# Linear attention in a two-layer block: level products over all 128 rows with a zeroed key operand, one masked copy a level, and no context outputs in the last layer

## What is computed

```python
def step(state, inp):                       # scanned over chunks, both directions
    qc, kc, vc, gc = inp
    b = jnp.cumsum(gc, axis=2)
    rel = jnp.exp(jnp.where(lower, b[:, :, :, None, :] - b[:, :, None, :, :], -jnp.inf))
    att = jnp.einsum('bhtk,bhsk,bhtsk->bhts', qc, kc, rel)
    o = (jnp.einsum('bhtk,bhkv->bhtv', qc * jnp.exp(b), state)
         + jnp.einsum('bhts,bhsv->bhtv', att, vc))
    ...
oc_f, sc_f = gla_chunked(pc['gq'], pc['gk'], pc['gv'], pc['gf'], zero_state)
ol_f, _ = gla_chunked(pl['gq'], pl['gk'], pl['gv'], pl['gf'], sc_f)
...
gla_lat = gla_output(ol_f + ol_b, pl['go'], gla_norm_g[layer])
if not last:
    gla_ctx = gla_output(oc_f + oc_b, pc['go'], gla_norm_g[layer])
```

## Time and profile before

| | |
|---|---|
| median of 3 runs | 4480.63 us (4475.74 to 4485.02) |
| profiled execution, time and span | 4477.87 us, 4476.0 us |
| mean granted TensorE clock | 0.888 of 2.4 GHz |
| linear attention, layer 0 and layer 1 (first head's diagonal to the last copy's end) | 227.1 and 235.4 us |
| DMA over the span | 71 GB/s |

### The profile page before, as it was taken

One profiled execution on the slowest core, in us unless ns is written; L12 is line 12 of the kernel. 1 busy time (PEld: TensorE's weight loads), 2 busy tenths in 40 slices (PEclk: granted clock), 3 DMA queues, 4 the chain that ended last, 5 costly groups with the idle time before them and its releaser, 6 DMA issues. The chain is left out here.

```text
span 4476.0 us, 53765 instructions
## 1 busy us (share of the span) xinstructions
PE 3734.3 (83%) x20722; PEld 3001.0 (67%) x20722; DVE 1757.0 (39%) x2589; ACT 1242.4 (28%) x2146; POOL 1248.0 (28%) x877
## 2 busy tenths in 40 slices
PE   6899596895786999999976697796959669999992
PEld 2588486673465888888861585685746458888881
DVE  2105543785563221221228014543967442122215
ACT  2211332674533111111004211432746331111111
POOL 1211321122334323323223211321214343333331
PEclk8999676797997999999998898676989879999996
DMA  8322302104332111111115223202021321111112
GB/s 296 135 84 113 87 13 60 26 11 96 89 101 75 38 38 37 37 37 39 36 59 210 95 86 125 48 19 62 19 63 43 127 75 43 55 48 47 47 38 89
DMA packets 150919, 318.59 MB, mean 71 GB/s; under 512 B 11816, under 2 KB 72200, under 8 KB 150768
## 3 DMA queue, kind: packets, MB, share of 16 engines
q1 hardware_dynamic: 128016, 260.47, 18.4%
q10 hardware_dynamic: 18528, 41.97, 2.5%
q0 software_dynamic: 4224, 14.09, 1.1%
HBM read 250.20 MB, written 66.29 MB: 71 GB/s over the span
## 5 line engine op out<-in xcount | busy, mean ns | idle before, releaser
L2006 POOL TENSOR_TENSOR ffn_wlo<-ffn_raw,ffn_whi 128x1024 fp32r<-128x1024 f32 x132 | 314.7, 2392 | 800.1 <-ACT ffn_whi L1977 800.1
L2070 DVE TENSOR_TENSOR ffn_hid<-ffn_up,ffn_silu 128x512 f32<-128x512 f32 (+1 forms) x110 | 70.2, 638 | 1048.9 <-PE ffn_up L127 1022.7
L1977 ACT CAST ffn_whi<-ffn_raw 128x1024 fp32r<-128x1024 f32 x132 | 136.4, 1049 | 944.6 <-PE ffn_acc L127 467.4
L2075 DVE TENSOR_TENSOR y<-ffn_acc,y 128x512 f32<-128x512 f32 x396 | 273.9, 692 | 266.7 <-PE ffn_acc L127 266.7
L125 PE MATMUL ffn_gate<-second_uhi,ffn_whi 128*128 128x512 f32 (+1 forms) x880 | 325.7, 370 | 37.3 <-POOL ffn_wlo L2006 37.3
L126 PE MATMUL ffn_gate<-second_ulo,ffn_whi 128*128 128x512 f32 (+1 forms) x880 | 325.3, 370 | 0.0
L127 PE MATMUL ffn_gate<-second_uhi,ffn_wlo 128*128 128x512 f32 (+1 forms) x880 | 325.1, 369 | 0.0
L126 PE MATMUL ffn_up<-second_ulo,ffn_whi 128*128 128x512 f32 (+1 forms) x880 | 323.9, 368 | 0.0
L125 PE MATMUL ffn_up<-second_uhi,ffn_whi 128*128 128x512 f32 (+1 forms) x880 | 323.8, 368 | 0.0
L127 PE MATMUL ffn_up<-second_uhi,ffn_wlo 128*128 128x512 f32 (+1 forms) x880 | 323.7, 368 | 0.0
L125 PE MATMUL ffn_acc<-ffn_whi,ffn_hhi 128*128 128x512 f32 x792 | 308.2, 389 | 0.0
(11 more groups left out here) (265 smaller groups left out, 8785.6 us busy)
## 6 DMA issues: line engine op xcount, KB each, us to landing
ffn_raw<-w_ffn_dram SPq DMA_DIRECT2D x132, 512.0 KB, 3.3
in_raw<-w_in_dram SPq DMA_DIRECT2D x42, 512.0 KB, 3.3
norm_input_ada_w<-w_ada_dram SPq DMA_DIRECT2D x10, 2048.0 KB, 8.2
norm_ffn_ada_w<-w_ada_dram SPq DMA_DIRECT2D x8, 2048.0 KB, 8.1
proj_scratch<-in_stage ACTq DMA_DIRECT2D x20, 640.0 KB, 2.9
ada_w<-w_ada_dram SPq DMA_DIRECT2D x6, 2048.0 KB
...
```

Of the source, the lines that this page charges most:

```text
L1977: act.copy(whi[:, j % 3, :], raw[:, j % 3, :]).then_inc(w_hi, 1)
L2006: pool.tensor_tensor(wlo[:, j % 3, :], raw[:, j % 3, :], whi[:, j % 3, :].bitcast(F32), ALU.subtract).then_inc(w_ready, 1)
L2070: dve.tensor_tensor(hf[:, c, 0:tn], UP[:, c, 0:tn], sg[:, c, 0:tn], ALU.mult).then_inc(mul_done, 1)
L2075: dve.tensor_tensor(Y[:, tt, cols], ACC[:, half, :], Y[:, tt, cols], ALU.add).then_inc(y_added, 1)
```

## The change

Each level becomes one matmul a chunk over all 128 rows. The moving operand is X as it is, 128 columns. The stationary operand is a copy XK of X in which the queries are set to zero: in the lower halves the rows DOWN, in the upper halves the rows UP. ScalarE makes XK with two activations a level (`key_parts`), each a copy with a scale of one or zero per partition (`side`, set by three small memsets on GpSimd). XK is a ring of 2. The product has the forward and the backward blocks in one 128x128 square per chunk, beside blocks that nothing reads, and takes the unit's banks from their start, so `level` has no wait for a bank. One predicated copy of 128x1280 under a mask of 128x128 takes the blocks of a level into A where two of 128x640 did.

In layer 1 (C0 = 2) levels, diagonal, output, mean, root, gate and store leave out the two context chunks, and so do the distances and exponentials of steps 1 to 4. Keys, states, XAB and the distances of step 0 stay whole, since the states need them.

```diff
+        C0 = CTX_TILES if layer == LAYERS - 1 else 0
+        ASKED = range(C0, NCH)
+        NA, t0 = NCH - C0, C0 * P
...
+        XK = sb(nm + "XK", [P, 2, T])
+        side = sb(nm + "side", [P, 2])
...
-        masks = sb(nm + "masks", [P, 10, HALF], I32)
+        masks = sb(nm + "masks", [P, 5, P], I32)
...
-                    plan(("level", h, l), "dve", 2)
+                    plan(("level", h, l), "dve", 1)
...
-        pieces = [[range(4 * k, min(4 * k + 4, NCH)) for k in range(3)] if g % STEPS == 4 else [range(2 * k, 2 * k + 2) for k in range(PAIRS)]
-                  for g in range(NS)]
+        def pieces_of(p):
+            first, n = (0, 2) if p == 0 else (C0, 4 if p == 4 else 2)
+            return [range(c, min(c + n, NCH)) for c in range(first, NCH, n)]
+        pieces = [pieces_of(g % STEPS) for g in range(NS)]
...
+            pool.memset(side[:, :], 0.0).then_inc(side_set, 1)
+            pool.wait_ge(side_set, 1)
+            pool.memset(side[UP, 0:1], 1.0).then_inc(side_set, 1)
+            pool.wait_ge(side_set, 2)
+            pool.memset(side[DOWN, 1:2], 1.0).then_inc(side_set, 1)
+            pool.wait_ge(side_set, 3)
...
-                for c in range(NCH):
-                    x = X[:, v % RING, chunk(c)]
-                    if c == 8:
-                        pe.wait_ge(bank_left, left(("level", h, l)) + 1)
-                    pe.matmul(fslot(s, c), x[UP, :], halves(x, m)[UP, :, 1, :], start=True, stop=True)
-                    mm = pe.matmul(bslot(s, c), x[DOWN, :], halves(x, m)[DOWN, :, 0, :], start=True, stop=True)
-                    if c == 1:
-                        mm.then_inc(bank_left, 1)
+                pe.wait_ge(key_part, 2 * (v + 1))
+                for c in ASKED:
+                    mm = pe.matmul(U[:, s, chunk(c)], XK[:, v % 2, chunk(c)], X[:, v % RING, chunk(c)], start=True, stop=True)
                 mm.then_inc(unit_done, 1)
...
+            def key_parts(g, k):
+                if g >= NS or k >= len(levels_of(g)):
+                    return
+                h, l = g // STEPS, levels_of(g)[k]
+                m, v = LEVELS[l], level_number(h, l)
+                if v == 0:
+                    act.wait_ge(side_set, 3)
+                act.wait_ge(x_pool, x_count(h, l))
+                act.wait_ge(x_dve, x_count(h, l))
+                if v >= 2:
+                    act.wait_ge(unit_done, made(("level",) + divmod(v - 2, len(LEVELS))))
+                for half in range(2):
+                    act.activation(halves(XK[:, v % 2, t0:], m)[:, :, half, :], halves(X[:, v % RING, t0:], m)[:, :, half, :],
+                                   ACT.Copy, scale=side[:, half:half + 1]).then_inc(key_part, 1)
...
                 h, p = divmod(g, STEPS)
+                key_parts(g, 1)
                 exponential(g + 2, 0)
                 exponential(g + 2, 1)
...
+                key_parts(g + 1, 0)
                 exponential(g + 2, 3)
...
-                shape = [P, NCH, HALF // m, m]
-                for d in range(2):
-                    dve.wait_ge(dve_took, taken(name) - 2 + d)
-                    data = U[:, s, 0:T // 2] if d == 0 else U[:, s, 3 * BANK - T // 2:3 * BANK]
-                    mask = masks[:, 2 * (l - 2) + d:2 * (l - 2) + d + 1, :].rearrange("p a (n m) -> p a n m", m=m).to_broadcast(shape)
-                    dve.copy_predicated(A[:, h % 2, :, :].rearrange("p c (n a m) -> p c n a m", a=2, m=m)[:, :, :, 1 - d, :], mask,
-                                        data.rearrange("p (c n m) -> p c n m", c=NCH, m=m)).then_inc(dve_took, 1)
+                dve.wait_ge(dve_took, taken(name) - 1)
+                mask = masks[:, l - 2:l - 1, :].to_broadcast([P, NA, P])
+                dve.copy_predicated(A[:, h % 2, C0:, :], mask, U[:, s, t0:T].rearrange("p (c n) -> p c n", n=P)).then_inc(dve_took, 1)
```

67 lines of the change are left out of this document (33 added, 34 removed).

## The result

The changed kernel takes **4347.92 us** (median of 4 runs, 4346.66 to 4350.14), the kernel before 4478.18 beside it (4461.47 to 4485.02): ratio 0.9715, 95% interval 0.9688 to 0.9742. The forecast was 4380, its range 4360 to 4440. The direction was right, the gain too small: the profiled spans differ by 127.7 us (4476.0 and 4348.3) where the sum had 101.

The account below looks back on a forecast made before the run. The prediction took TensorE to set the length of the linear attention heads. Clock gains of 33 us (layer 0) and 41 (layer 1) plus 27 for fewer chunks made 101 off a 4476.0 span: median 4380, range 4360 to 4440.

Parts of the forecast that it names:

- What bounds it: Linear attention's heads in both layers: TensorE sets their length, busy 208.6 of layer 0's 227.1 us.
- an unmoved clock: Rival, TensorE in the heads: clock not lifted by streamed columns, heads alternate as before; 4443 us, chance 0.13.
- a load that is not hidden: Rival, level matmuls: weight load no longer hidden, a level about twice 2.45 us; 4502 us, chance 0.04.
- The clock: TensorE in the heads: levels streaming 128 columns run at 1.00 but for short falls; 33 us layer 0, 41 layer 1.
- Fewer chunks in layer 1: Layer 1's levels, diagonal, output and distances of steps 1 to 4 on 8 of 10 chunks: 27 us.
- The sum: Whole kernel: 33 + 41 + 27 = 101 us off a span of 4476.0, predicted median 4380.
- 44.0 for a plain head: Layer 0 heads without mean and root: 44.0 us, from head 0's 45.65 us once the wait before its output goes.
- 5 a layer for short falls: Taken back from each layer's clock gain: 5 us for short falls at the mean, the root and the tail.
- I take no difference at equal clock: A level's matmuls on TensorE: new form costs the same as the old 2.45 us; range -0.05 to +0.1 us a level.
- The masked copy: VectorE, five levels a head: one copy of 128x1280 for two, taken at 1.75 us, bounds 1.49 and 3.23.
- The key parts: ScalarE, two activations a level: 0.69 us each, 0.57 in layer 1, costed at nothing because of ScalarE's slack.
- ScalarE is late: Rival: key parts at 1.2 us (1.0 in layer 1) give TensorE gaps and more falls; 4421 us, chance 0.10.

Follow-up runs that it names:

- b_exp_first: Kernel before, with only the fifth exponential of a step moved on ScalarE ahead of level 1's copies, the squares and the square root: 4391.26 us.
- b_fewer_gap: Kernel before with only layer 1's chunks dropped, plus one wait a head put back there (step 2's second distances wait for level 1's copies): 4450.59 us.
- b_128_columns: Kernel before, with each level matmul on 64 rows streaming 128 columns instead of 64, results overwriting each other: 4419.63 us.
- a_gap: Changed kernel with a wait put into layer 1: step 2's second distances wait for ScalarE's copies of level 1: 4348.48 us.
- a_all_chunks: Changed kernel with all ten chunks again in layer 1: 4381.75 us.
- a_two_copies_1: Changed kernel with each level of steps 2 to 4 copied out by two masked copies, as before, instead of one: 4370.72 us.
- a_keys_doubled: Changed kernel with every key part made twice on ScalarE, each level waiting for both: 4395.78 us.

## Why the prediction was wrong

**What bounds it: right.** TensorE set the length of the heads, and the clock was the largest item. A level of 20 records took 2.39 us, copies 1.63, and the rivals of an unmoved clock and of a load that is not hidden both fell: the four levels in a row took 9.51 us at 1.00. The Trainium skill, TensorE: Matmul & The Clock Gate, part 2, step 1, says that a load's time goes with its columns and not with its rows; the trace agrees: at clock 1.00 a load of 64 rows and 128 columns took 0.188 us (the old levels), one of 128 rows and 128 columns 0.192 (the new ones), and one of 128 rows and 64 columns 0.137 (A times V).

**"The clock": the effect right, half of its cause missing.** Plain heads at 1.00 were foreseen, and came. But the prediction asked what TensorE did before a rise and took the answer, streamed columns, as the whole cause. It did not ask what it did before a fall. The 0.95 us wait stood in the earlier trace rows and was priced at its own length. Runs b_exp_first and b_fewer_gap show that it started falls; the waits and what they set off were worth 84 us in the kernel before. The half of the cause that was named is true: b_128_columns gains 52 us (4471.79 to 4419.63), and a_gap shows that the new levels bear such a wait. The rule of the Trainium skill that the prediction weighed and set aside (part 1 of the same page: gaps between bursts lose the clock) is borne out in its first half, by pauses of 0.6 to 2.2 us. Its other half, that keeping busy brings it back, is not: 17.34 us of levels and 34.15 us of levels and distances in the windows above, both without a pause, stayed at 0.50. The rival built on it gave 4443 because it too counted only the length of the waits. None of this moved the forecast's number: behind the new levels a wait brought only short falls.

**"Fewer chunks in layer 1": right in work, blind to the wait.** 7.1 us a plain head were foreseen; at clock 1.00 in both layers of a_all_chunks a plain head is 40.5 to 40.6 us and layer 1's in the changed kernel 32.75 and 33.33, so 7.3 to 7.7. But the term left out that four pieces of distances in place of five take the wait away. Added to the old kernel, this part alone gave 75.6 us of the median (4483.02 to 4407.40). The sum lost nothing by it, since the new levels claim the same clock: the two causes overlap in layer 1, and either alone would have done.

**The sum: the step that failed.** What put the time below the range is the price of a plain head at full clock, "44.0 for a plain head". It measured 40.5 to 40.6 us. The account closes head by head: the heads lost 31 us more than the sum had. In layer 0 they lost 3.5, 16.0, 12.5 and 11.1 us where 1.7, 12.7, 13.6 and 10 were foreseen, in layer 1 23.9, 20.5, 24.5 and 20.4 where the terms with 7.1 for the chunks are 19.8, 16.9, 20.7 and 17.1. The four plain heads make 13 of the 31. Another 11 were taken back (5 a layer for short falls, 1 for ScalarE): layer 0's last two heads, short falls and all, took 101.1 us where the terms had 52 and 49.2 before anything was taken back, so that was once too many. The last 7 are layer 1's last two heads, among them the wait of 2.43 us that layer 0's third head still has. The bounds allowed for no shorter plain head, which is why the lower end, 4360, was missed too. What the 44.0 and the other terms left out:

- "I take no difference at equal clock", range -0.05 to +0.1 us a level. It was about -0.3 by the starts, outside that range, and not in the records but in the borders: 7 x 0.3 is 2.2 us a head. The prediction compared a level's first start with its last end, 2.45 by 2.40, where start to next start tells the cost.
- The plain head at 1.00. The 44.0 was head 0's 45.65 less its wait, but that head holds a fall of 3.4 us, worth 1.7. With this and the borders it comes to 40.1; a new wait of 0.6 to 0.7 us for an exponential in step 1 makes it 40.8, and the plain heads of a_all_chunks are 40.5 and 40.6.
- The masked copy, 1.75 taken, 1.63 measured. Its worth was set at the old wait of 1.7 us a plain head; a_two_copies_1 shows 2.2 and 3.8 in layer 0's plain heads and 5.1 and 4.5 in layer 1's shorter ones.

**The key parts: size wrong, verdict nearly right.** 0.846 and 0.735 us measured, 0.69 and 0.57 taken (bounds 0.6 and 1.0). They cost 5 us in the heads and 7.7 in the median, not nothing. The rival "ScalarE is late" needed 1.2 us each; a_keys_doubled, at 1.7 for each half, costs 48 us, by waits in ScalarE's order and not by a full ScalarE.
